# Input projection of a hybrid decoder layer: from one level of Strassen's algorithm to two, with the outer sums on GpSimd

## The reference, cut to what matters

```python
h = rms_norm(x, mix_norm_w[l])          # x: (1, 2048, 1024)
z = h @ w_in[l]                         # w_in: (1024, 7424)  ->  z: (2048, 7424), float32
sq, sk, sv, rq, rk, rv, rg, mq, zg = split_cols(z, IN_SIZES)
# ... window attention, retention, memory attention, gates, output projection,
# ... then 32 experts, 4 of them for each token
```

## Time and profile before

| | us |
|---|---|
| median of three runs | 4644.1 (4643.5 to 4646.4) |
| span of the profiled execution | 4643.7 |
| norm_inputs, to its last transposed sum | about 59 |
| project_inputs, first to last matmul | 66.1 to 1200.3 |
| mix_tokens to run_experts | the rest, from 1202.9 |

### The profile page before, as it was taken

How to read it: one execution, slowest core, us unless ns; L and a number is a source line. 1 busy time by engine, 2 the same in 40 slices (tenths; PEclk the granted TensorE clock), 3 DMA queues, 4 the chain that set the end, 5 groups by cost and what they waited for, 6 DMA issues and landing times.

```text
span 4643.7 us, 96160 instructions
## 1 busy us (share of the span) xinstructions
PE 4540.3 (98%) x29134; PEld 4181.9 (90%) x29135; DVE 2959.4 (64%) x5657; ACT 2193.7 (47%) x4265; POOL 457.5 (10%) x488
## 2 busy tenths in 40 slices
PE   6999999999899999999899999999999999999998
PEld 5888888888688778788899999999999999999998
DVE  7555565555599733456677777777666666565664
ACT  5212232222388622222566666666555555555554
POOL 0000000000143100012111011101010101010100
PEclk7999999999999999999999999999999999999999
DMA  5232342333455534444577677667575757565655
GB/s 200 104 123 98 115 169 104 109 110 108 157 185 182 193 137 149 158 150 135 173 227 220 213 226 224 207 213 213 183 216 178 216 179 215 177 207 178 196 174 139
DMA packets 573587, 796.68 MB, mean 172 GB/s; under 512 B 51760, under 2 KB 516144, under 8 KB 566512
## 3 DMA queue, kind: packets, MB, share of 16 engines
q1 hardware_dynamic: 548704, 716.96, 46.0%
q0 software_dynamic: 24720, 77.67, 7.4%
HBM read 644.74 MB, written 149.75 MB: 171 GB/s over the span
## 4 chain that ended last, share of the span: by engine, by line
PE 51%; DMA 0%; issue 0%; DVE 0%; ACT 0%; DVEq 0%; POOLq 0%; POOL 0%; SPq 0%; ACTq 0%
PE e_acc L2950 12%; PE e_acc L2951 12%; PE e_acc L2952 12%; PE e_acc L2944 8%; PE e_acc L2945 4%; PE e_yp L2918 1%; PE e_xT L2908 1%; PE e_acc L2948 1%; PE e_acc L2947 1%; DMA e_raw<-in_w_up 0%; DMA e_xg<-h,e_rec_in 0%; DVE e_wlo L2792 0%; DVEq L2501 0%; DMA e_rec_in<-slots 0%; ACT e_whi L2659 0%
## 5 line engine op out<-in xcount | busy, mean ns | idle before, releaser
L2792 DVE TENSOR_TENSOR e_wlo<-e_raw,e_whi 128x512 fp32r<-128x512 f32 x1548 | 1046.1, 686 | 389.0 <-ACT e_whi L2659 366.0
L2659 ACT CAST e_whi<-e_raw 128x512 fp32r<-128x512 f32 x1548 | 950.2, 650 | 24.9 <-issue 10.3
L637 PE MATMUL p_acc<-p_hi,a_hi 128*128 128x464 f32 x1792 | 670.3, 374 | 10.5 <-DVE p_lo L527 10.5
L639 PE MATMUL p_acc<-p_hi,a_lo 128*128 128x464 f32 x1792 | 669.1, 373 | 0.0
L638 PE MATMUL p_acc<-p_lo,a_hi 128*128 128x464 f32 x1792 | 666.8, 372 | 0.0
L2950 PE MATMUL e_acc<-e_x_both,e_whi 128*128 128x264 f32 (+6 forms) x2176 | 640.6, 294 | 0.0
L2952 PE MATMUL e_acc<-e_x_both,e_whi 128*128 128x264 f32 (+6 forms) x2176 | 637.8, 293 | 0.0
L2951 PE MATMUL e_acc<-e_x_both,e_wlo 128*128 128x264 f32 (+6 forms) x2176 | 637.7, 293 | 0.0
L2950 PE MATMUL e_acc<-e_ahi,e_whi 128*128 128x264 f32 (+11 forms) x2048 | 594.0, 290 | 0.3 <-DVE e_alo L2837 0.3
L2952 PE MATMUL e_acc<-e_alo,e_whi 128*128 128x264 f32 (+11 forms) x2048 | 584.3, 285 | 0.0
L2951 PE MATMUL e_acc<-e_ahi,e_wlo 128*128 128x264 f32 (+11 forms) x2048 | 584.1, 285 | 0.0
(11 more groups left out here) (379 smaller groups left out, 7773.5 us busy)
## 6 DMA issues: line engine op xcount, KB each, us to landing
e_raw<-in_w_up SPq DMA_DIRECT2D x1036, 256.0 KB
e_raw<-in_w_down SPq DMA_DIRECT2D x512, 256.0 KB
p_raw<-in_w_in SPq DMA_DIRECT2D x64, 928.0 KB, 4.6
z<-p_z SPq DMA_DIRECT2D x32, 928.0 KB, 4.0
z<-p_u SPq DMA_DIRECT2D x32, 928.0 KB, 3.9
b_gates<-z SPq DMA_DIRECT2D x16, 1536.0 KB
oT<-x_oT SPq DMA_DIRECT2D x16, 1024.0 KB, 9.8
b_raw<-oT SPq DMA_DIRECT2D x15, 1024.0 KB
```

What stands on the lines that cost most here:

```text
L637: pe.matmul(out, a_hi[:, j, at], hi[:, k, :], start=k == 0, stop=False)
L639: mm = pe.matmul(out, a_lo[:, j, at], hi[:, k, :], start=False, stop=k == HALF_K - 1)
L2659: act.copy(held(w_hi, u), loaded(u)).then_inc(hi_made.sem, 1)
L2792: dve.tensor_tensor(held(w_lo, u), loaded(u), held(w_hi, u).bitcast(F32), ALU.subtract).then_inc(lo_made.sem, 1)
```

## The change

The whole matrix product is divided twice by the same algorithm. The outer level works on quarters of 1024 tokens x 512 and of 512 x 928 weights; the inner level divides each of the outer products again, into blocks of 512 tokens x 256 and 256 x 464. There are 4 groups of 1856 columns, 7 outer products in each and 7 inner products in each of these: 196 inner products (`ROUNDS`) of 4 token blocks x 2 chunks x 3 passes = 24 matmuls of 464 columns.

- The inner products are added up partly in PSUM (an accumulation group goes on over several products). Each is then taken in one instruction of 128x1856: by ScalarE as a copy for Q1, Q6, Q5 and Q4, by VectorE as an addition for Q2, Q7 and Q3. A set of four banks is free again when this one instruction has ended.
- Both operands are split for every inner product: 128x928 of weights and 128x1024 of tokens, the high parts on ScalarE and the low parts on VectorE.
- The sums of inner weight blocks (`mix`, 4 for each outer product, 128x928) and of outer weight blocks (`mix_outer`, 16 rows of 128x928 for each group) are VectorE's.
- The outer sums of results (`combine`, 128x1856) and the sums of token blocks (`combine_s`, 128x1024) are GpSimd's, but S3 and S1 of three outer products of each group, which VectorE makes.
- `norm_inputs` stores all the token blocks of the outer level as they are (`a` is now 7 x 4 x 128 x 1024), and `project_inputs` loads four blocks of 512 KB for each outer product.
- `mix_tokens` waits for stores of z at two places in SyncE's queue. The scratch space for GpSimd's DMAs is set to 8192.

```diff
-PAIRS_IN = 4
-SWEEPS = TILES // (2 * PAIRS_IN)
+G = 464
+BLOCKS = 4
 PRODUCTS = 7
+GROUPS = ZW // WIDE
+QUADS = 4
+SUB = QUADS * 2 * P
+HELD_UNITS = 5
+OUTER = PRODUCTS * GROUPS
+ROUNDS = OUTER * PRODUCTS
+P1, P2, P6, P7, P5, P3, P4 = range(PRODUCTS)
+Q1, Q2, Q6, Q5, Q7, Q3, Q4 = range(PRODUCTS)
...
+    def by_scalar(j):
+        return j in (Q1, Q6, Q5, Q4)
...
         @blk.scalar
+            def split(n):
+                o, j = Steps.split(n)
+                if n >= 2:
+                    act.wait_ge(summed.sem, n - 1)
...
+                wait_moving(act, o, j)
+                act.copy(inputs.w_hi[n % 2][:], moving(o, j)).then_inc(w_hi_made.sem, 1)
+                wait_stationary(act, o, j)
+                act.copy(inputs.a_hi[n % 2][:], stationary(o, j)).then_inc(a_hi_made.sem, 1)
+            def take(n):
...
+                wait_unit_free(act, o, x)
+                act.wait_ge(summed.sem, n + 1)
+                act.copy(unit(o, x)[:], sums(n)).then_inc(taken_act.sem, 1)
+            split(0)
+            for n in range(ROUNDS):
+                if n + 1 < ROUNDS:
+                    split(n + 1)
+                if n > 0:
+                    take(n - 1)
...
         @blk.vector
+            def split(n):
+                o, j = Steps.split(n)
+                dve.wait_ge(w_hi_made.sem, n + 1)
+                dve.tensor_tensor(inputs.w_lo[n % 2][:], moving(o, j), inputs.w_hi[n % 2][:].bitcast(F32),
+                                  ALU.subtract).then_inc(w_lo_made.sem, 1)
+                dve.wait_ge(a_hi_made.sem, n + 1)
+                dve.tensor_tensor(inputs.a_lo[n % 2][:], stationary(o, j), inputs.a_hi[n % 2][:].bitcast(F32),
                                   ALU.subtract).then_inc(a_lo_made.sem, 1)
+            def add(n):
...
+                held = unit(o, x)[:]
+                dve.tensor_tensor(held, held, sums(n), ALU.add).then_inc(taken_dve.sem, 1)
...
+            for n in range(ROUNDS):
+                o, j = Steps.split(n)
+                g, outer = divmod(o, PRODUCTS)
+                if n + 1 < ROUNDS:
+                    split(n + 1)
+                if n > 0:
+                    add(n - 1)
+                first = (P2, P2, P6, P7) if g == 0 else (P1, P2, P6, P7)
...
+                if j == Q1:
+                    mix(o, T1)
+                if j == Q5:
+                    mix(o, T4)
+                if o + 1 < OUTER:
+                    if j == Q7:
+                        mix(o + 1, T3)
+                    if j == Q4:
+                        mix(o + 1, T2)
+                    if j == Q3 and outer >= P5:
+                        combine_s(o + 1)
...
+        @blk.gpsimd
+            def combine(o, x):
+                g, outer = divmod(o, PRODUCTS)
+                if outer == P1:
+                    return
+                if x == C21:
+                    pool.wait_ge(taken_act.sem, Steps.taken(Steps.product(o, Q4), True))
+                else:
+                    j = {C11: Q2, C22: Q7, C12: Q3}[x]
+                    pool.wait_ge(taken_dve.sem, Steps.taken(Steps.product(o, j), False))
...
+                elif outer == P5:
+                    pool.tensor_tensor(a[:], a[:], new[:], ALU.add).then_inc(done.sem, 1)
+                    pool.wait_ge(done.sem, Steps.combined(o) - 1)
+                    pool.tensor_tensor(new[:], new[:], b[:], ALU.add).then_inc(done.sem, 1)
...
+            def combine_s(o, s):
...
+                elif s == S2:
+                    pool.wait_ge(a_lo_made.sem, Steps.product(o, Q1) + 1)
+                    pool.wait_ge(s_made[S1].sem, o + 1)
+                    ins = pool.tensor_tensor(sub(a11), sub(a21), sub(a11), ALU.subtract)
...
+            for o in range(OUTER):
+                outer = o % PRODUCTS
+                if o > 0:
+                    combine(o - 1, C12)
+                    if outer == P3:
+                        combine_s(o, S4)
+                    combine(o - 1, C21)
+                if outer != P3:
+                    combine_s(o, S4)
+                combine(o, C11)
+                if o + 1 < OUTER and outer < P5:
+                    combine_s(o + 1, S3)
+                    combine_s(o + 1, S1)
+                combine(o, C22)
+                if o + 1 < OUTER:
+                    combine_s(o + 1, S2)
...
         @blk.tensor
+            for n in range(ROUNDS):
+                pe.wait_ge(w_lo_made.sem, n + 1)
+                pe.wait_ge(a_lo_made.sem, n + 1)
+                opens = j in (Q1, Q2, Q5)
+                if n >= 2:
+                    scalar = Steps.by_scalar((n - 2) % PRODUCTS)
+                    taken = taken_act if scalar else taken_dve
+                    pe.wait_ge(taken.sem, Steps.taken(n - 2, scalar))
+                for q in range(QUADS):
+                    for k in range(2):
+                        pe.matmul(out, a_hi[:, at], hi[:, k, :], start=opens and k == 0, stop=False, skip_group_check=chained)
...
+            memory.wait_upper_written(sp)
             load(Tile(0, 0))
...
-    io["a"] = scratch("a", (PRODUCTS, P, PAIRS_IN * HALF_K * P))
+    io["a"] = scratch("a", (PRODUCTS, SUBS, P, SUB))
...
-    nc = _bacc.Bacc("TRN2", target_bir_lowering=False, num_devices=1)
+    nc = _bacc.Bacc("TRN2", target_bir_lowering=False, num_devices=1, dynamic_dma_scratch_size=8192)
```

More of the change, by code:

```diff
@@ L179, in norm_inputs @@
+def norm_inputs(nc, io, inputs, ident, eps):
+    XS = 7
     QUARTERS = 4
+    Q11, Q12, Q21, Q22 = range(QUARTERS)
+    S3, S1, S2, S4 = range(4)
     with ExitStack() as c:
[L181 to L185, removed]
@@ L188, in norm_inputs @@
+        pt = [c.enter_context(nc.psum_tensor(f"n_pt{i}", [P, 2, 512], F32)) for i in range(QUARTERS)]
         w_in_sb = Signal(io["sems"], nc, "n_w_in", 16)
@@ L234, in _ @@
                 sp.dma_start(xs[v % XS][:], io["x"][tile_of(v) * P:(tile_of(v) + 1) * P, :]).then_inc(x_in[v % XS].sem, 16)
[L235 to L239, removed]
+            inputs.load(sp, io, WA, 0)
+            for u in range(QUADS):
+                store(u)
+                if u < 2:
+                    inputs.store_far(sp, io, u, stack[u])
+            inputs.load(sp, io, WB, 0)
         @blk.gpsimd
@@ L244, in _ @@
             pool.memset(eps[:], EPS).then_inc(ident_made.sem, 1)
+            for u in range(QUADS - 1):
+                combine(pool, u, combined, 2 * u)
         @blk.scalar
@@ L259, in _ @@
             act.wait_ge(ident_made.sem, 3)
[L260 to L269, removed]
+            for v in range(QUARTERS):
+                root(v)
@@ L271, in _ @@
+            for u in range(QUADS):
+                for n, (q, out) in enumerate(((Q11, first(u)), (Q12, stacked(u, P2)), (Q22, stacked(u, P4)))):
+                    if u + 1 < QUADS:
+                        root(4 * (u + 1) + n)
+                        if n == 2:
+                            root(4 * (u + 1) + 3)
+                    act.wait_ge(turned.sem, turned.after(u, 4 if q == Q22 else 2))
+                    act.copy(out, quarter(q)).then_inc(copied.sem, 1)
         @blk.vector
         def _(dve):
[L273 to L281, removed]
@@ new lines, in store @@
+            def store(o, x):
+                g, outer = divmod(o, PRODUCTS)
+                m1, n1 = {P2: (0, 0), P5: (1, 1), P3: (0, 1), P4: (1, 0)}[outer]
+                m2, n2 = {C11: (0, 0), C12: (0, 1), C22: (1, 1), C21: (1, 0)}[x]
+                rows = slice((2 * m1 + m2) * QUADS * P, (2 * m1 + m2 + 1) * QUADS * P)
+                col = g * WIDE + (2 * n1 + n2) * G
+                k = Steps.held(o, x)
+                sp.wait_ge(combined[x].sem, Steps.combined(o))
+                sp.dma_start(io["z"][rows, col:col + G].rearrange("(q p) n -> p q n", p=P), inputs.unit[Steps.place(k)][:]).then_inc(
+                    memory.z_out[Steps.place(k)].sem, 16)
@@ new lines, in mix_outer @@
+            def mix_outer(g, i, row):
+                for slot in ((WC, WD), (), (), ())[i]:
+                    dve.wait_ge(inputs.w_in[slot].sem, 16 * (g + 1))
+                if i > 0:
+                    dve.wait_ge(outer_made.sem, outer_made.after(g, 4 * i))
+                    dve.wait_ge(w_lo_made.sem, Steps.product(g * PRODUCTS + i, Q1) + 1)
+                out, x, y, op = ((WD, WC, WD, ALU.subtract), (WA, WA, WD, ALU.add), (WB, WB, WA, ALU.subtract),
+                                 (WA, WC, WA, ALU.subtract))[i]
+                dve.tensor_tensor(inputs.w[out][:, row, :], inputs.w[x][:, row, :], inputs.w[y][:, row, :], op).then_inc(
+                    outer_made.sem, 1)
@@ new lines, in _ @@
+            split(0)
+            mix(0, T3)
+            mix(0, T2)
+            for n in range(ROUNDS):
+                o, j = Steps.split(n)
+                g, outer = divmod(o, PRODUCTS)
+                if n + 1 < ROUNDS:
[3 more added lines that the diff above has]
+                first = (P2, P2, P6, P7) if g == 0 else (P1, P2, P6, P7)
+                for i in range(4):
+                    if outer == first[i]:
```

(9 more changed lines are left out.)

737 lines of the change are left out of this document (414 added, 323 removed).

## The result

The changed kernel takes **5005.5 us** (5005.4 to 5006.3, four runs) against 4644.2: a ratio of 1.0774 (95% interval 1.0759 to 1.0789), slower by 361 us. The forecast was 4900 us, 4740 to 5030.

What follows compares the result with a forecast made beforehand. VectorE and GpSimd taking turns were to bound the projection: 208 + 163 - 21 - 5 = 345 us a group, 1380 for the stage; 4643.7 - 1134.2 + 1380 + 10 gave 4900 us, range 4740 to 5030.

Steps and rivals of the forecast that it cites:

- upper end: Projection stage: VectorE's 208 and GpSimd's 163 us a group all in a row, additions too, 1485 us for four groups.
- both ends: Start and end of the projection: first matmul 3 us later, last product +5; together +10 us (-5 to +30).
- What bounds it: Projection: two-SBUF-input instructions of VectorE and GpSimd run whole by turns, at least 309 us a group against TensorE's 248.
- The prices: Projection instructions: GpSimd's 1856 elements 4.03 us, ScalarE's copy 1.7, VectorE's addition 2.04, its low parts 1.08 and 1.18.
- The sum of VectorE and its blocking: Projection: VectorE 208 plus GpSimd 163, less 21 overlapped and 5 hidden, 345 us a group, 1380 for the stage.
- the two-deep buffers don't stretch the stage: Projection products: ScalarE's high parts are there 2 us after the product before the last ended, earlier than VectorE needs them.
- rival 2: TensorE's clock falls in the projection: 5345 us if for the whole stage; chance of more than 5030 us 0.05.
- sign of being right, clock 1.00: Profile after, projection: TensorE's granted clock stays at 1.00, the upper level (2.4 GHz).
- Rival 1: Projection: GpSimd's long sums don't stop VectorE, TensorE stays the bound, 4546 us in all; chance 0.09.
- The additions from PSUM are free of the turn-taking: Projection: VectorE's additions have one SBUF input and can run beside GpSimd's sums, near 2.1 us each.

Runs made afterwards that it cites:

- experiment 1: Changed kernel with GpSimd's sums of two tiles in the projection replaced by fills that write but don't read: projection stage 1072 us, against 1488.
- Experiments 7 and 8: Changed kernel with 21 (7) and 16 (8) matmuls in each product instead of 24: projection stage 1448 and 1404 us, against 1488.
- experiments 5 and 6: Changed kernel with idle 48-column TensorE matmuls, three before each of three waits (5), six and four before two (6): projection stage 1537 and 1517 us.

## Why the prediction was right, point by point

- **The number.** 4900 forecast, 5005.5 measured, inside the range by 25 us, and this in part by luck. The stage alone is 1488 us, 3 above the 1485 that I called its upper end; the range holds it because I had allowed 30 us for both ends, of which 7 were needed. That all in a row (1485) comes so near to 1488 is chance: VectorE was busy for 1359 us and idle for 130, and the 1485 have no idle time in them.
- **What bounds it.** Right. VectorE and GpSimd read by turns, and this took the place of TensorE's matmuls for most of the stage: VectorE is busy for 91% of it, TensorE for 77%. Instructions of 4 us do block one another whole (5.15 at 639.60), which the rows of before showed for 1.3 us only. By the Trainium skill (SBUF — State Buffer, Who interferes with whom) the shared interface is held for the whole instruction, and a GpSimd instruction that only writes leaves VectorE's two-input form alone. The trace agrees with the first (a subtraction of 1.1 us ends 1.08 after a sum of 4 us), experiment 1 with the second (1125 ns beside 611 us of writing).
- **The prices.** GpSimd's 1856 elements: 4.03 forecast; 4088 ns is the shortest of its rows after, 5.0 us the usual one, with a subtraction of VectorE before it. ScalarE's copy 1.7 (1699 ns), VectorE's addition 2.04 (2075), the low parts 1.08 and 1.18 (1.04 and 1.13 from start to start when not blocked). All within 5%. The 1.08 came from two subtractions from start to end (2.16); from start to start has 1.04.
- **The sum of VectorE and its blocking.** 1380 us forecast for four groups. VectorE's busy time in the stage is 1359:

```profile
66.93:1555.34 1488.41, 1141.56 (x4704) 967.84 (x4704) 1358.64 (x675) 553.84 (x505) 784.78 (x199) 0.88 0.29 100
```

  In experiment 1 the same 675 instructions, unblocked, took 817 (I had 832), so blocking took 542 us, 83% of GpSimd's 653 (4 x 163); I had 548, 84%.
- **The step that was mis-sized: idle time of VectorE.** I wrote that the two-deep buffers don't stretch the stage, because ScalarE's high parts would always be there first. They were not: VectorE is idle for 130 us of 1488 (total, times, longest):

```profile
DVE p_lo L714 <- ACT p_hi L676: 104.7, 68, 4.6
```

  105 of them are behind ScalarE's high part of the weights, which waits for the end of a product. 1380 - 21 (busy time over-estimated) + 130 is 1489, the stage. The mean of 7.0 us a product hid that rounds are uneven: when VectorE has been blocked twice in a round, TensorE pauses for up to 9.1 us and then needs its full product time before ScalarE may split again, while VectorE, with little to do in that round, waits. One such case, VectorE, TensorE, ScalarE, VectorE:

```profile
593.80 5.12 DVE L714 TENSOR_TENSOR p_lo<-p_wd,p_hi 128x928 fp32r<-128x928 f32 x1
598.84 5.12 DVE L717 TENSOR_TENSOR p_alo<-p_sub,p_ahi 128x1024 fp32r<-128x1024 f32 x1
...
604.06 0.73 PE L912 MATMUL p_acc<-p_hi,p_ahi 128*128 128x464 f32 x1 [6.20 <-issue]
...
612.11 0.97 ACT L676 CAST p_hi<-p_t 128x928 fp32r<-128x928 f32 x1 [10.70 <-PE p_acc L914]
...
613.11 1.12 DVE L714 TENSOR_TENSOR p_lo<-p_t,p_hi 128x928 fp32r<-128x928 f32 x1 [1.70 <-ACT p_hi L676]
```

  The product that starts at 604.06 lasts 8.0 us instead of 5.06, since two thirds of its matmuls start 0.39 us apart. With 5.06 it would have ended near 609.2 and the high part been ready about 1 us later, before VectorE was free at 611.4: this wait of 1.7 us is the clock's. Experiments 7 and 8 show that the length of the product matters in this way.
- **The clock (rival 2).** My sign of being right, clock 1.00, failed: it was 0.88, at the lower level after some of the pauses. It added 149 us to TensorE's own busy time (1142 us, where 4704 matmuls 0.211 apart are 992). Windows of 2 us around one pause (clock in the last column but two):

```profile
634.00:636.00 2.00, 0.42 (x3) 0.03 (x1) 2.00 (x1) 1.54 (x2) 1.56 (x1) 1.00 0.00 0
636.00:638.00 2.00, 0.00 (x0) 0.00 (x0) 2.00 (x2) 0.37 (x1) 0.00 (x0) 0.83 0.21 45
638.00:640.00 2.00, 1.21 (x3) 1.13 (x4) 2.00 (x3) 0.00 (x0) 1.28 (x1) 0.50 0.64 225
640.00:642.00 2.00, 2.00 (x6) 1.68 (x6) 2.00 (x1) 0.00 (x0) 2.00 (x1) 0.50 0.00 0
642.00:644.00 2.00, 2.00 (x7) 1.69 (x6) 2.00 (x1) 0.00 (x0) 1.67 (x1) 0.50 0.00 0
644.00:646.00 2.00, 2.00 (x11) 1.80 (x10) 2.00 (x2) 0.00 (x0) 1.17 (x1) 0.96 0.00 0
```

  TensorE stands still from 634.4 to 638.8, the grant falls from the upper level (2.4 GHz) to the lower (1.2) at about 637, and comes back near 644. Here 6 or 7 matmuls start in 2 us instead of 11. The rows that I took as evidence had the same busy share, 69 and 73%, but I had not looked at how long their pauses were; a share doesn't tell that. How much of the 130 us is the clock's stays open: experiments 5 and 6 could not hold it. An estimate: experiments 7 and 8 took 115 and 279 us off TensorE's busy time and the stage fell by 41 and 84, so 149 us, if each is worth as much, are some 50 of the stage.
- **Both ends.** +10 forecast, +0.8 and +6.0 measured.
- **Rival 1 (TensorE stays the bound).** Refuted for this kernel. Its price was 46 to 55 us too low: without GpSimd's reading the stage is 1072 to 1081 where it had 1026.
- **The additions from PSUM are free of the turn-taking.** Held: 2077 ns in the mean among subtractions with a mean of 2332, and 2082 in experiment 1.

## What to carry to other kernels

Two engines that are both below the bound by their busy time can be above it together: where rows show that their instructions take turns, add their times before comparing with the bound. Before moving elementwise work with two inputs in SBUF from VectorE to GpSimd, look whether VectorE's own work also has two inputs there; here each sum handed over cost its own 4 us instead of 2, and taking all of them back gave 257 us. When the bound moves to a chain of engines with uneven rounds, an average per round is a lower end and not the forecast: give the idle time a term of its own (here 130 us on 1359), and look at the longest pauses of TensorE, not at its share, before trusting its clock.

## What the runs showed of the hardware

- GpSimd filling tiles for 611 us of 1072 leaves VectorE's subtractions with two SBUF inputs at 1125 ns (128x928); with GpSimd summing two tiles, busy or blocked for 785 us of 1488, those of 128x928 take 2332 in the mean.
- Bringing 1 MB for each product, at 277 GB/s with the engines 76% busy and issued from ScalarE's queue at 0.33 us each, cost TensorE no wait in 147 products.
- In TensorE's pause from 634.4 to 638.8 its granted clock fell from the upper level to the lower, and near 644, with TensorE at work since 638.8, it was back at the upper.
